# A hybrid decoder step: sample tokens of the linear attention as a tile of their own, state products in two column tiles, tail scores with heads innermost, row maxima on both sides of the combination

## What is computed

```python
z = rms_norm(h, norm_w) @ w_in          # dq, dk, dv, dg | gq, gk, gv, gg, ga
# group A: differential attention, 4 heads, two maps each
a = softmax(q @ k.T * scale + rel_bias) # causal, for both maps
p = a[map 0] - lam * a[map 1]
o_d = p @ v
# group B: gated linear attention (GLA), 4 heads, in chunks
b = cumsum(lg)                          # log decays within the chunk
o_inter = (q * exp(b)) @ S
A = einsum(q, exp(b_t - b_s), k)        # causal within the chunk
o_g = o_inter + A @ v
S_new = exp(b_last) * S + (k * exp(b_last - b)).T @ v
# both
mix = [rms_norm(o_d) * silu(dg), rms_norm(o_g) * silu(gg)]
y = h + mix @ w_out
```

## Time and profile before

| | us |
|---|---|
| median of three runs | 1144.21 |
| the three runs | 1138.04 to 1147.42 |
| the profiled execution, its own time | 1142.4 |
| span of its trace | 1140.7 |
| TensorE busy in the span | 949.7 (83%) |
| VectorE / ScalarE / GpSimd busy | 580.2 / 462.1 / 278.2 |
| second stage in the trace | about 696 to 1029 |
| third stage | about 1029 to 1141 |

### The profile page before, as it was taken

One profiled execution on the slowest core, in us unless ns is written; L12 is line 12 of the kernel. 1 busy time (PEld: TensorE's weight loads), 2 busy tenths in 40 slices (PEclk: granted clock), 3 DMA queues, 4 the chain that ended last, 5 costly groups with the idle time before them and its releaser, 6 DMA issues. The chain is left out here.

```text
span 1140.7 us, 23645 instructions
## 1 busy us (share of the span) xinstructions
PE 949.7 (83%) x8207; PEld 745.4 (65%) x8207; DVE 580.2 (51%) x985; ACT 462.1 (41%) x1251; POOL 278.2 (24%) x436
## 2 busy tenths in 40 slices
PE   4898899887999988798889993467777798856998
PEld 3897699555676555566666783356666677535886
DVE  4777552554455343445554424466688884345221
ACT  4744342322233332323434342456678763214100
POOL 1010300223332321233222203564564621000000
PEclk9999999999999989899999997577899999867999
DMA  7456933889899777899889625411212200007231
GB/s 216 140 167 194 363 105 92 293 315 346 285 314 350 258 256 236 287 330 333 308 289 316 228 77 160 149 43 52 70 52 56 59 24 10 1 8 245 91 111 51
DMA packets 139315, 207.56 MB, mean 182 GB/s; under 512 B 21314, under 2 KB 83388, under 8 KB 139196
## 3 DMA queue, kind: packets, MB, share of 16 engines
q1 hardware_dynamic: 118300, 138.39, 37.4%
q0 software_dynamic: 20832, 67.60, 17.3%
q10 hardware_dynamic: 64, 0.07, 0.0%
HBM read 181.54 MB, written 24.45 MB: 181 GB/s over the span
## 5 line engine op out<-in xcount | busy, mean ns | idle before, releaser
L553 POOL DMA_DIRECT2D vraw<-in_cache_v x256 | 137.3, 536 | 513.7 <-PE po L919 436.5
L823 PE MATMUL pz<-wh,xTh 128*128 128x256 f32 (+1 forms) x576 | 174.8, 303 | 3.6 <-DVE wl L1014 3.6
L1097 DVE STREAM_TRANSPOSE kx<-kraw 128x2048 f32<-128x2048 f32 x64 | 147.6, 2307 | 45.5 <-DMA kraw<-in_cache_k 44.6
L823 PE MATMUL pz<-wh,xTl 128*128 128x256 f32 (+1 forms) x576 | 165.0, 286 | 0.0
L823 PE MATMUL pz<-wl,xTh 128*128 128x256 f32 (+1 forms) x576 | 164.8, 286 | 0.0
L823 PEld LDWEIGHTS pz<-wh,xTh 128*128 128x128 f32 (+1 forms) x576 | 108.6, 189 | 36.4 <-issue 23.9
L823 PEld LDWEIGHTS pz<-wh,xTl 128*128 128x128 f32 (+1 forms) x576 | 109.0, 189 | 0.0
L823 PEld LDWEIGHTS pz<-wl,xTh 128*128 128x128 f32 (+1 forms) x576 | 108.6, 188 | 0.0
L819 PE MATMUL pz<-xTh,wh 128*128 128x384 f32 (+1 forms) x288 | 101.1, 351 | 0.0
L1674 PE MATMUL pS<-ks,qs 128*128 128x512 f32 (+5 forms) x288 | 79.6, 430 | 20.6 <-DVE bl L2179 19.3
L819 PE MATMUL pz<-xTh,wl 128*128 128x384 f32 (+1 forms) x288 | 95.0, 330 | 0.0
(11 more groups left out here) (230 smaller groups left out, 1861.2 us busy)
## 6 DMA issues: line engine op xcount, KB each, us to landing
kraw<-in_cache_k SPq DMA_DIRECT2D x256, 256.0 KB, 5.5
vraw<-in_cache_v POOLq DMA_DIRECT2D x256, 256.0 KB, 5.3
wraw<-in_w_in SPq DMA_DIRECT2D x112, 128.0 KB, 5.5
out<-nat SPq DMA_DIRECT2D x32, 128.0 KB, 3.4
wraw_o<-in_w_out SPq DMA_DIRECT2D x8, 512.0 KB, 5.0
vraw<-in_x_prompt SPq DMA_DIRECT2D x7, 512.0 KB, 4.0
xr<-in_x_prompt SPq DMA_DIRECT2D x7, 512.0 KB, 3.6
out<-xr SPq DMA_DIRECT2D x7, 512.0 KB, 2.6
```

What stands on the lines that cost most here:

```text
L553: pool.dma_start(vraw[:, t % VR, n, :], page_rows(cache_v, page)).then_inc(v_in[t % VR], 16)
L823: ins = pe.matmul(z[0:r, 0:CB], a[:, k, P * x:P * x + r], b[:, w, :], start=(n == 0), stop=(n == 3 * KT - 1))
L1097: dve.transpose(kx[:, GRP * g:GRP * g + GRP, :].rearrange("p n x -> p (n x)"), kraw[:, t % KR, :, :].rearrange("p n x -> p (n x)")).then_i ...
```

## The change

1. The GLA now has ten positions, `gorder = [0, 1, "S", 2, ..., 8]`. Position 2 is the 32 sample tokens alone (`PS`); the tail tile at the end has only the 16 prompt tokens. The 49 steps are dealt out over the half rounds by the same rule, so nearly all move: several tiles now have A0 and A1 in the same round, where before most had them in two.
2. In `g_output` the samples' heads go to column tiles of 32 (`tile_position=(0, 32 * h)`), state after state with the heads innermost. The masked queries `q8` live in `mixT`, the masked keys `kd8` in the memory of the last four value tiles, whose loads are issued after the samples' states are done (in round 12).
3. In `g_state` each head has a product of its own with 64 columns of weights, two beside each other in column tiles of 64, so that one head pair fills 128 partitions; VectorE updates a state in two instructions of 128x128 in place of four of 64x128. This holds for every tile and every sample state.
4. In `scores` the tail unit issues each kind of product for all four heads before the next kind.
5. VectorE takes the maximum of map 0 of unit `u` ahead of `combine(u - 1)`, and that of map 1 behind it; the tail unit keeps both behind.
6. Loads: only `mask` is waited for by the first mask; the sample states are waited for in step KO of position 1; the values come in three groups. `dd` and `ff` lie in a tensor `spare` that outlives the stage, and the first four slices of `w_out` are loaded into it at the end of the second stage, ahead of the stores of the states.

```diff
+            gorder = [0, 1, "S"] + list(range(2, TILES))
+            for p in range(NG_):
+                steps += [(x, p) for x in ("A0", "A1", "KO", "DS", "MX") if x != "A1" or gorder[p] in range(TILES - 1)]
...
                 sp.wait_ge(mix_done, TILES - 1)
                 sp.dma_start(ob[S0:S0 + NS, :], od_d).then_inc(od_in, 16)
                 load_gate(TILES - 1)
-                load_gg(TILES - 1)
-                sp.wait_ge(sdn, TILES + NB)
+                load_gg(NG_ - 1)
+                sp.wait_ge(dexp, NG_)
+                sp.wait_ge(kdt, NG_ - 1)
+                for k in range(4):
+                    sp.dma_start(spare[:, k * D:(k + 1) * D], w_out[0, k * P:(k + 1) * P, :]).then_inc(wo_in[k], 16)
+                sp.wait_ge(sdn, states_done(NG_ - 1))
...
+                            for hh in heads:
+                                product(0, hh)
+                            if n0 < n1:
+                                for band in (bh, bl):
+                                    for hh in heads:
+                                        pe.matmul(pS[rows(hh), s0 + n0:s0 + n1], typed(turn_hi[:, 0:nq]),
+                                                  typed(band[:, hh, c]), start=False, stop=False,
+                                                  tile_position=(0, rows(hh).start))
+                            for hh in heads:
+                                ins = product(1, hh)
...
+                    if p == PS:
                         pe.wait_ge(q8d, 1)
+                        for c in range(NB + 1):
+                            for h in range(H):
+                                if c == 0:
+                                    a, b = at[0:r, h % 2, h // 2, 0:r], vg[0:r, p % 2, h * DV:(h + 1) * DV]
+                                else:
+                                    a, b = q8[:, h % 2, h // 2, c - 1, :], ss_[:, c - 1, h // 2, :]
+                                ins = pe.matmul(gA[32 * h:32 * h + 32, 1, 0:DV], a, b, start=(c == 0), stop=(c == NB),
+                                                tile_position=(0, 32 * h))
...
+                        for m in range(2):
+                            for hh in range(2):
+                                k = kd8[:, c, m * P + DK * hh:m * P + DK * hh + DK] if p == PS else kd[0:r, m, own[hh]]
+                                h = 2 * m + hh
+                                ins = pe.matmul(gA[own[hh], c % 2, m * P:(m + 1) * P], k,
+                                                vg[0:r, p % 2, h * DV:(h + 1) * DV], start=True, stop=True,
+                                                tile_position=(0, DK * hh))
...
-                            dve.wait_ge(g_in, 16 * 6)
                             factors(0)
...
                 for u in range(NU + 1):
+                    if u < NU and u != LAST0:
+                        maximum(u, 0)
                     if u >= 1:
                         combine(u - 1)
+                    if u == LAST0:
+                        maximum(u, 0)
                     if u < NU:
-                        maxima(u)
+                        maximum(u, 1)
                     g_step(2 * u)
...
             def load_w(k):
-                    if k >= 4:
-                        sp.wait_ge(wol_d, k - 3)
+                    sp.wait_ge(wol_d, k - 3)
...
-                for k in range(KT):
+                for k in range(4, KT):
                     load_w(k)
```

More of the change, by code:

```diff
@@ L1232, in hymba_kernel @@
         g_out = sem("g_out")
+        spare = sb(ctx, "spare", [P, 3 * 5 * 4 * P])
+        wo_in = [sem(f"wo_in{n}") for n in range(4)]
         with ExitStack() as st:
@@ new lines, in load_values @@
+                def load_values(i):
+                    n = P if i < TILES - 1 else TAIL
+                    sp.dma_start(vd[0:n, i, :], v_prompt.rearrange("a b l h d -> (a b l) (h d)")[P * i:P * i + n, :])\
+                      .then_inc(b_in[v_group[i]], 16)
+                def g_step(s):
+                    for x, p in g_at(s):
+                        if x == "A0" and p + 2 < NG_:
+                            load_g(p + 2)
+                        if x == "KO" and 1 <= p and p + 1 < NG_:
+                            load_vg(p + 1)
+                            load_gg(p)
+                        if x == "MX" and p == PS:
+                            sp.wait_ge(dsd, states_done(PS))
+                            for i in range(TILES - 4, TILES):
+                                load_values(i)
@@ new lines, in scores, with rows, product @@
+                            heads = range(H) if tail(u) else [h]
+                            typed = (lambda a: a.bitcast(F32)) if tail(u) else (lambda a: a)
+                            def rows(hh):
+                                return slice(32 * hh, 32 * hh + 32) if tail(u) else slice(0, P)
+                            nq = 32 if tail(u) else P
+                            def product(x, hh):
+                                return pe.matmul(pS[rows(hh), s0 + k0:s0 + k1], typed(qs[:, i % 2, m, x, hh, 0:nq]),
+                                                 typed(ks[:, m, hh, k0:k1]), start=(x == 0), stop=(x == 1),
+                                                 tile_position=(0, rows(hh).start))
@@ L1775, in g_state @@
+                        if p:
+                            ins = pe.matmul(to, qz[:, p % 2, h % 2, h // 2, 0:r], sp_[:, h // 2, :], start=False, stop=True)
+                    ins.then_inc(ogd, 1)
+                def g_state(p):
+                    r = g_rows(p)
+                    pe.wait_ge(kdo, p + 1)
+                    if p == PS:
+                        pe.wait_ge(kd8d, 1)
+                        pe.wait_ge(ogc, p + 1)
+                    for c in range(NB if p == PS else 1):
                         if c >= 2:
-                            pe.wait_ge(sdn, i + c - 1)
```

496 lines of the change are left out of this document (230 added, 266 removed).

## The result

| | median, us | range, us | ratio to before, 95% interval |
|---|---|---|---|
| before, in the same series | 1141.99 | 1138.04 to 1147.42 | |
| after | 1163.97 | 1162.34 to 1167.53 | 1.0193 [1.0141, 1.0246] |

The changed kernel is 1.9% slower; 1.2% faster was forecast, and the time lies above the range. The profiled execution took 1167.5 us, with a span of 1165.9 against 1140.7.

The account below looks back on a forecast made before the run. The prediction saw a loop over engines, little bound by one engine, and a serial tail. Its terms summed to -14.3 us, giving 1130 us for the median, 1.2% below 1144.21; the forecast's own range was 1119 to 1140.

Parts of the forecast that it names:

- Start, -5: Start of the stage: factors no longer wait for the sample states' load, so the first combination comes 4.8 us earlier.
- The tail, -9, -3 and -15.3: Tail unit: output products 9 us less, scores 3 us less, the chain from scores to combination 15.3 us less.
- Loads of w_out, -1: Third stage's start: ScalarE's wait for the first slice goes, four load issues delay the block's end; net 1 us less.
- The samples in the middle, +13: Rounds 10 and 11: the samples' work moved there takes 14.6 us, of which 2 is hidden; 13 us more.
- What goes from the middle, -7: Middle rounds: masked queries leave round 29 and state updates become fewer; 7 us less together.
- The states' part, -4: Middle rounds: eight states at two updates in place of four, 5.6 us with some in slack; 4 us less.
- The masked queries, -3: Round 29: four masked queries, 3.5 us, no longer stand ahead of a combination; 3 us less.
- Other places of the steps, -4: Tile rounds: masks wait less for their products, which in five tiles now come right behind the turn; 4 us less.
- The maximum ahead of the combination, +17: Every round: the first maximum delays the combination and so TensorE's turn; 17 us more, ends 0 and +30.
- Rival C: Rounds of 640 and 768 keys: TensorE's idle time lowers its clock, 15 us more; 1162 us, chance 0.08.
- rival B: The maximum costs all it can, 30 us, and the new places of the steps give nothing; 1147 us, chance 0.18.

Follow-up runs that it names:

- x_maxold: Changed kernel with both maxima behind the combination again, as before the change; all else as changed: 1127.24 us, ratio 0.9865 to before.
- x_noprefetch: Changed kernel with all of w_out loaded in the third stage again: 1165.91 us, ratio 1.0180 to before.
- x_best1: Changed kernel with both maxima behind the combination and the w_out loads at the start of the third stage again: 1125.18 us, ratio 0.9844 to before.
- b_places: Kernel before with only the new dealing of the GLA steps, the samples' places left empty and the samples still in the tail: 1157.94 us, ratio 1.0117.
- b_state2: Kernel before with only the state products in two column tiles and two state updates of 128x128 in place of four of 64x128: 1135.13 us, ratio 0.9934.
- y_ex2: Changed kernel with old maxima order, state stores ahead of early loads, tile steps in their old half rounds, samples in round 10: 1133.83 us, ratio 0.9883.
- b_wait: Kernel before with the combination also held until the next unit's map 0 scores are there, both maxima behind it: 1162.78 us, ratio 1.0148.
- x_best2: Changed kernel with both maxima behind the combination and the state stores ahead of the four early w_out loads: 1123.55 us, ratio 0.9819.

## Why the prediction was wrong

- **Start, -5: right.** From VectorE's copy that opens the stage (701.96, 704.31 and 697.82) to the first combination pass 25.9 us before, 22.2 after and 22.0 in `x_maxold`, 4 us less.
- **The tail, -9, -3 and -15.3: right in the sum, in part by luck.** From unit 31 to unit 32 are 26.8 us less than before (28.0 in `x_maxold`). What stands behind the scores gave 15.5, as forecast. The output products gave 6.5 in place of 9, since I priced them at the full clock and it was 0.50; the scores gave 6.5 in place of 3; and the weighing between them took 3.3 us in place of 1.9, at a clock of 0.55.
- **Loads of w_out, -1: the wrong sign.** The trace behind the last combination is 3.4 us longer than before, and the undoing of the loads takes 1.4 us off it in `x_noprefetch` and 4.2 in `x_best1`. The step took the stores behind the four loads at their price before.
- **The samples in the middle, +13: near.** `b_places` has the same places without the samples. From unit 9 to 14 `x_maxold` takes 18 us more, but in this stretch it also has the factors of tile 2 (2.29 and 2.55 us, from 776.98 on), which `b_places` has ahead of unit 9. From unit 0 to 14 it takes 14.7 more, what my working gives if nothing is hidden; I had let 2 us be hidden.
- **What goes from the middle, -7: less than half is there.** The states' part, -4, is 1 us by `b_state2`: slack. The masked queries, -3, weren't tried alone, but `y_ex2` has the tiles' steps where they were before: its rounds of units 29 and 30 take 14.5 us, 16.4 in `b_state2` and 16.7 before. So they give some 2 us.
- **Other places of the steps, -4: failed.** I looked only at the wait for products that goes when A0 and A1 share a round, not at KO and DS, which do so too. Alone it costs 12 us. The parts don't simply add: from unit 14 to 31 `b_places` costs 20 us, and the whole change with the old maxima 5; what makes the 15 us between them I only infer (cheaper updates, no masked queries, a clock of 0.96 against 0.93).
- **The maximum ahead of the combination, +17: this decided.** It is 37 us in the changed kernel and 49 in the kernel before. The step had the mechanism right and even an upper end of 30, and then took a bit over the middle, for a cover that I gave too much weight: I said that in rounds where VectorE is busy the maximum has only changed places. In those rounds themselves that is nearly so, 3.1 us for four of them. But such a long round is followed by a short one, in which the combination needn't wait for new scores; the new order takes just that away, as in the round of unit 22, and the four rounds behind the long ones cost 14.3. With 37 in place of 17 the sum would come to 1150; the other 14 us up to the measured time belong to the terms above, the places of the steps before all.
- **Rival C had the other half.** I priced the clock at 15 us, in the rounds of 640 and 768 keys, at a chance of 0.08 and only on top of rival B. Its 1162 us lie near the measured 1164, and its sign came true (0.87), but part of that is luck: the longer records are 9.4 us over the 17 rounds from unit 14 to 31, not 15 in eight of them, and what is left is longer waits. The clock belonged in the sum: for each microsecond that TensorE waits longer its records are longer by half a microsecond (9.4 beside 21.5 us, the changed kernel against `x_maxold`) to nearly two (13.1 beside 7.3, `b_wait`). In the kernel before the mean clock from unit 14 to 31 falls from 0.99 to 0.90 by the wait alone.

The Trainium skill, "TensorE: Matmul & The Clock Gate", section "What's actually happening", says that being slow is the default state and that activity releases it. The traces agree: the same 38 records take 5.06 us at 1.00 and 7.98 us at 0.76 behind a longer wait.

## What to carry to other kernels

A wait put ahead of the one instruction on which a full engine's next work hangs costs time in every round, and here TensorE's longer records cost half of the idle time to twice as much on top; price both, and look for rounds that are short only because the other engine had worked ahead. When steps are dealt out anew, count for each round what stands ahead of its critical instruction, not only whether a step comes earlier. And a gain of one engine is worth its full size where the work is serial and next to nothing where there is slack: the shorter state update was worth 9.7 us at the tail and 1 in the loop.

## What was not expected of the hardware

- A store's issue on SyncE's queue takes longer behind issued loads: 1.99 and 3.41 us for the stores of `state_p` behind four loads of `w_out`, 0.58 and 0.67 us ahead of them in `x_best2`.
- VectorE's instructions with two inputs are at times twice as long beside GpSimd. The same combination of 768 keys takes 1.02 us in some rounds and 2.10 in others; the two factors of the position behind the samples take 2.29 and 2.55 us in the changed kernel, from 787.85 on, and 1.23 and 1.48 from 740.05 on, where GpSimd is idle. GpSimd was at work for 9.5 of 10 us around them:

```profile
784.00:794.00 10.00, 4.04 (x82) 3.05 (x80) 7.92 (x9) 8.23 (x25) 9.53 (x8) 0.80 0.15 34
```

The Trainium skill, "SBUF — State Buffer", section "SBUF: two separate sides", calls the port pair of the two engines an exclusive lock and not a bandwidth split. The trace agrees that instructions with two inputs are the ones that stretch: the maxima, with one, took 0.94 to 0.96 us in the same rounds. Work of GpSimd at the same time isn't enough, though. The combination at 897.29 that takes 2.10 us begins while GpSimd's instructions from 895.98 on run. The one at 920.59 takes 1.02, though GpSimd begins an instruction of line 1636 during it; that one takes 1.01 us, and 0.30 at 904.48. Both fit a lock that goes to the one that begins first. What the samples' rounds would take without GpSimd's work beside them wasn't tried.
